# Experts loop: the rounding of the activated tile moves to ScalarE, its lower part moves one weight part later, and the positions of four experts are compared in one operation

## The reference, cut to what matters

```python
expert = grp[:, None] * EXPERTS_PER_GROUP + top_idx          # two experts for each token
h_pad = jnp.concatenate([h, jnp.zeros((1, d), h.dtype)], axis=0)
xb = h_pad[slot_tok].reshape(n_blocks, MOE_BLOCK, d)         # tokens gathered by expert
def run_block(args):
    xe, e = args
    return (jax.nn.silu(xe @ w_gate[e]) * (xe @ w_up[e])) @ w_down[e]
y = jnp.zeros((n_tok + 1, d)).at[slot_tok].add(yb * slot_gate[:, None])
```

## Time and profile before

| | us |
|---|---|
| three runs | 2054.73, 2055.91, 2060.94 |
| median | 2055.91 |
| span of the profiled execution | 2060.3 |
| busy in that span: PE, PEld | 1914.5, 1749.8 |
| busy in that span: DVE, ACT | 1423.0, 1168.0 |
| experts loop, first to last YE operation of passes 0 to 29 | 483.28 |

### The profile page before, as it was taken

One profiled execution on the slowest core, in us unless ns is written; L12 is line 12 of the kernel. 1 busy time (PEld: TensorE's weight loads), 2 busy tenths in 40 slices (PEclk: granted clock), 3 DMA queues, 4 the chain that ended last, 5 costly groups with the idle time before them and its releaser, 6 DMA issues.

```text
span 2060.3 us, 30308 instructions
## 1 busy us (share of the span) xinstructions
PE 1914.5 (93%) x12946; PEld 1749.8 (85%) x12946; DVE 1423.0 (69%) x1424; ACT 1168.0 (57%) x1310; POOL 76.5 (4%) x94
## 2 busy tenths in 40 slices
PE   6999998998998989998998999898789999999997
PEld 5989998997997979998997999796778888888785
DVE  4687548546555677637745555757679999999995
ACT  3553344544444554334644444465388888888883
POOL 0000013000000000013000000000000000000000
PEclk9999999998999999999998999999789999999998
DMA  8334374543554433356534555333269999999993
GB/s 307 121 116 149 128 255 164 205 143 143 186 183 144 159 144 133 131 179 237 213 139 150 184 184 184 139 117 122 111 256 376 377 377 377 372 380 372 374 396 131
DMA packets 64524, 440.87 MB, mean 214 GB/s; under 512 B 7372, under 2 KB 7372, under 8 KB 14592
## 3 DMA queue, kind: packets, MB, share of 16 engines
q1 hardware_dynamic: 55296, 399.63, 51.4%
q0 software_dynamic: 8096, 35.30, 4.7%
q10 hardware_dynamic: 992, 3.93, 0.5%
HBM read 428.61 MB, written 10.23 MB: 213 GB/s over the span
## 4 chain that ended last, share of the span: by engine, by line
PE 66%; DVE 21%; ACT 8%; issue 2%; POOL 1%; DMA 1%; DVEq 0%; ACTq 0%; POOLq 0%
PE psum L188 65%; DVE ring_low L202 6%; ACT hl L198 3%; DVE arena L212 3%; DVE ht L202 2%; DVE rounded L202 2%; DVE rounded L212 2%; PE psum L192 2%; DVE arena L202 1%; POOL arena L202 1%; ACT arena L198 1%; DVE hl L202 1%; ACT rounded L198 1%; ACT gn L198 1%; DVE resid L202 1%
## 5 line engine op out<-in xcount | busy, mean ns | idle before, releaser
L202 DVE TENSOR_TENSOR hl<-ring,hl 128x2048 fp32r<-128x2048 f32 (+1 forms) x190 | 433.7, 2286 | 316.7 <-ACT hl L198 316.3
L188 PE MATMUL psum<-ht,hl 128*128 128x256 f32 x4992 | 628.9, 287 | 7.5 <-DVE ht L202 7.5
L188 PEld LDWEIGHTS psum<-ht,hl 128*128 128x128 f32 x4992 | 614.6, 195 | 17.8 <-DVE ht L202 9.5
L198 ACT ACTIVATE hl<-ring 128x2048 fp32r<-128x2048 f32 (+1 forms) x286 | 536.4, 1895 | 116.9 <-PE psum L188 110.1
L198 ACT ACTIVATE arena<-psum 128x512 f32<-128x512 f32 (+5 forms) x232 | 120.9, 521 | 419.9 <-PE psum L188 395.3
L188 PE MATMUL psum<-hl,ax 128*128 128x512 f32 (+1 forms) x1608 | 351.9, 355 | 6.2 <-DVE ax L202 4.8
L188 PEld LDWEIGHTS psum<-hl,ax 128*128 128x128 f32 x1608 | 264.4, 191 | 47.5 <-DVE ax L202 5.5
L202 DVE TENSOR_TENSOR ring_low<-ring,hl 128x2048 fp32r<-128x2048 f32 x96 | 215.3, 2285 | 19.0 <-ACT hl L198 18.8
L188 PE MATMUL psum<-arena 128*128 128x128 f32 (+6 forms) x1520 | 190.1, 291 | 14.4 <-ACT arena L198 7.9
L188 PEld LDWEIGHTS psum<-arena 128*128 128x128 f32 (+2 forms) x1520 | 174.9, 180 | 25.1 <-ACT arena L198 8.7
L188 PE MATMUL psum<-hl,ht 128*128 128x256 f32 (+1 forms) x1056 | 138.4, 296 | 16.0 <-DVE ht L212 14.0
(11 more groups left out here) (121 smaller groups left out, 1890.1 us busy)
## 6 DMA issues: line engine op xcount, KB each, us to landing
ring<-W SPq DMA_DIRECT2D x284, 1024.0 KB, 5.1
arena<-W SPq DMA_DIRECT2D x48, 1024.0 KB, 7.8
ht_raw<-W SPq DMA_DIRECT2D x46, 1024.0 KB, 7.8
gate_d<-arena POOLq DMA_DIRECT2D x32, 256.0 KB, 3.8
arena<-gate_d POOLq DMA_DIRECT2D x8, 1024.0 KB, 9.3
gn<-GB POOLq DMA_DIRECT2D x10, 512.0 KB, 4.1
arena<-GB POOLq DMA_DIRECT2D x6, 512.0 KB, 5.1
ring<-W SPq DMA_DIRECT2D x4, 512.0 KB, 5.3
```

The costliest lines, as they stand in the source:

```text
L188: return Nothing() if self.e is None else self.e.matmul(o, a, b, start=start, stop=stop, skip_group_check=skip_group_check)
L198: return self.e.activation(o, a, f, bias=bias, scale=scale)
L202: return Nothing() if self.e is None else self.e.tensor_tensor(o, a, b, op)
```

## The change

Four edits, all in `few()` and its constants:

1. The copy that rounds hid into the upper part of aT leaves VectorE. ScalarE does it in a new step `upper_hid(e)` between the SE copy and the next two uppers. It waits for VectorE's "hid" of the same expert, and for TensorE's down(e-2).
2. The subtraction for the lower part of aT (`lower_hid`) moves on VectorE behind one more lower; it waits for ScalarE's new copy.
3. The wait for down(e-2) moves with the copy from VectorE to ScalarE.
4. `prep` becomes one operation of 128x1024 in place of four of 128x256. `iota` grows from 64 to 128 columns (the constants by 32 KB), and both of TensorE's waits are now for the end of the one operation.

```diff
-                   ("tri_ge", 128), ("iota", 64), ("fold", 64), ...
+                   ("tri_ge", 128), ("iota", 128), ("fold", 64), ...
...
-    put("iota", np.tile(np.arange(CAP, dtype=np.float32), (128, 1)))
+    put("iota", np.tile(np.arange(CAP, dtype=np.float32), (128, 2)))
...
-                    pe.wait_ge(s_dve, V["oh2", g])
+                    pe.wait_ge(s_dve, V["oh", g])
...
+                def upper_hid(e):
+                    ac.wait_ge(s_dve, V["hid", e])
+                    if e >= 2:
+                        ac.wait_ge(s_pe, P["ye", e - 2])
+                    act(mo.aT[e % 2][:, :, 0, :], mo.hid.rearrange("p (k n) -> p k n", k=4), ACT.Copy, "aT", e, after=False)
...
                     if e < 31:
                         place(e + 1)
+                    upper_hid(e)
                     cut(2)
...
-                    for s in range(2):
-                        for t in range(2):
-                            tt(mo.OH[g % 2][:, t, :].rearrange("p (e s n) -> p e s n", e=4, s=2)[:, :, s, :],
-                               posm[:, t, 4 * g:4 * g + 4].unsqueeze(2).broadcast_to([128, 4, 64]),
-                               C("iota").unsqueeze(1).broadcast_to([128, 4, 64]), ALU.is_equal, ("oh", "oh2")[s], g, after=False)
+                    tt(mo.OH[g % 2].rearrange("p t (e n) -> p t e n", e=4),
+                       posm[:, :, 4 * g:4 * g + 4].unsqueeze(3).broadcast_to([128, 2, 4, 128]),
+                       C("iota").unsqueeze(1).unsqueeze(1).broadcast_to([128, 2, 4, 128]), ALU.is_equal, "oh", g, after=False)
...
                 def turn_(e):
                     ve.wait_ge(s_act, A["sg", e])
                     tt(mo.hid, mo.sg, half(beside, 1), MUL, "hid", e)
-                    if e >= 2:
-                        ve.wait_ge(s_pe, P["ye", e - 2])
+
+                def lower_hid(e):
                     hi, lo = (mo.aT[e % 2][:, :, s, :] for s in range(2))
-                    hid = mo.hid.rearrange("p (k n) -> p k n", k=4)
-                    copy(hi, hid)
-                    tt(lo, hid, hi.bitcast(F32), SUB, "aT", e)
+                    ve.wait_ge(s_act, A["aT", e])
+                    tt(lo, mo.hid.rearrange("p (k n) -> p k n", k=4), hi.bitcast(F32), SUB, "aT", e, after=False)
...
                     turn_(e)
-                    cut(4)
+                    cut(1)
+                    lower_hid(e)
+                    cut(3)
```

More of the change, by code:

```diff
@@ L34 @@
 SHAPE_COLS = Cols([("ident", 128), ("rev", 128), ("rot", 128), ("bones", 128), ("ones", 128),
-                   ("tri_ge", 128), ("iota", 64), ("fold", 64), ("s_lt_t", 128), ("s_le_t", 128),
+                   ("tri_ge", 128), ("iota", 128), ("fold", 64), ("s_lt_t", 128), ("s_le_t", 128),
                    ("lev", 7 * 128), ("rowf", 2), ("eps6", 1), ("eps5", 1), ("eps64", 1), ("tiny", 1)])
```

## The result

| | before | after |
|---|---|---|
| median of 4 runs, us | 2058.43 | 2117.95 |
| lowest to highest | 2054.73 to 2062.27 | 2116.55 to 2119.86 |
| span of the profiled execution | 2060.3 | 2114.7 |
| YE operation of pass 0 to that of pass 29 | 483.28 | 537.89 |

The ratio is 1.0301 (95% interval 1.0283 to 1.0319): 59.5 us slower. Forecast were 57.5 slower and 2113.4, with a range of 2105 to 2129. Of the 23 runs of the kernel before that stand beside the last four variants, one took 6458.61 us; the ratios leave it out.

What follows compares the result with a forecast made beforehand. Bound: a circle of waits through TensorE's gather, ScalarE's copies and upper, VectorE's lowers and YE operation. Terms: 29 passes +52.5, pass 0 +2.4, pass 30 +2.1, first gather +0.45; together +57.5, 2113.4 us, range 2105 to 2129.

Steps and rivals of the forecast that it cites:

- hid at S+5.78, the stall, the hand-over: From YE operation start S: hid starts at 5.78, ScalarE stands about 2.1 us, hand-over from VectorE takes 0.04.
- The copy's price: ScalarE's new 128x256 copy rounding hid takes 0.26 us in its queue, with ends of 0 and 0.40.
- The plain pass: Experts-loop pass with gather and without prep, YE operation to YE operation: 18.31 us against 16.58, +1.73.
- With prep: Six passes in which prep stands ahead of hid: 18.31 + 1.15 = 19.46 us against 17.10.
- Without gather: Passes 27 to 29, bounded by VectorE's route to lower 12: 17.60 us against 15.79.
- The wide comparison: Prep's one operation of 1024 elements lasts 1.226 us, 1.15 in the queue, with ends of 0.9 and 1.4.
- What is next late: Slack beside the new circle: VectorE ready for lower 12 0.7 us early; TensorE needs about 16.25 of 18.31.
- Ahead of the loop: First gather waits for the whole wide prep operation, 1.23 us instead of about 0.77: about +0.45.
- a whole rival: TensorE's clock falls at new gaps; two falls a pass add 1.5 in 29 passes, total 2157; chance 0.09.
- a clock of 1.00 over the loop: Sign of a right forecast: TensorE's granted clock stays at 1.00 (2.4 GHz) throughout the experts loop.
- no stall: ScalarE finds hid done, if ready by S+4.5; plain passes stay 16.58, total 2053.3; chance 0.06.
- VectorE's work sets the pass: VectorE's work sets every pass; what it sheds, 17.3 us, comes off, giving 2038.6; chance 0.03.

Runs made afterwards that it cites:

- the last four variants: Hid one lower sooner 2058.99 us, prep as one operation only 2055.69, gu one upper later 2044.11, gather between the halves 2045.16; kernel before beside them 2057.81.
- lower part at once: The changed kernel with the lower part of aT right behind hid on VectorE, not one lower later: 2114.99 us.

## Why the prediction was right, point by point

- **hid at S+5.78, the stall, the hand-over.** In the changed kernel hid starts at 1743.63 with S at 1737.85: 5.78. The copy starts 0.04 after hid ends (1744.05 to 1744.09), the value taken from between 0.02 and 0.11. The profile puts the idle at 1.99, where the walk had 2.11 from the earliest next start; the rest is the SE copy's own tail.
- **The copy's price**, taken as 0.26 between 0 and 0.40: it is 0.32 from start to start (1744.09 to 1744.41). That term is 0.06 too small, and the whole pass came out only 0.03 longer than the sum.
- **The plain pass**, 18.31: measured 18.33 to 18.35. **With prep**, 19.46: 19.46 or 19.47. **Without gather**, 17.60: 17.64.
- **The wide comparison**, 1.226 less an overlap: it lasts 1.22 or 1.23, and broadcast operands make no difference.
- **What is next late.** VectorE at lower 12 was to wait 0.7; it waits 0.62. TensorE is off the circle with gaps of about 1 us before down, 0.8 before turn and 1.83 to 1.88 before down with prep; the forecast had 1.1 to 1.4, about 1, and 2.2 to 2.5.
- **Ahead of the loop.** The first gather starts 1.38 after the start of prep where it was 0.90, 0.48 later (forecast 0.45). From hid to the YE operation of pass 0 it is 12.63 (forecast 12.53).
- **The total.** Head apart (below), from the first operation of prep to the end it is 564.1 before (2060.3 - 1496.24) and 625.5 after (2114.7 - 1489.21): +61.4 where the terms summed to +57.5. The missing 3.9, all but 0.1 of it: plain passes 20 x 0.03 = 0.6; no gather 0.1; pass 1 with 18.95, 0.6; the pass behind prep three times 18.6, 0.8; pass 30, forecast 14.20 + 2.14 = 16.34, measured 17.89, 1.5; pass 31, 0.2.
- **The mis-sized term** is thus mainly the clock. I had counted its fall as a whole rival, twice in each pass, or as nothing, and named a clock of 1.00 over the loop as a sign of being right. Up to pass 30 it fell in a few single places: in pass 0, in three of the six passes with prep (15, 19 and 23), in pass 27, and in pass 30. The one in pass 0 isn't new: the kernel before has it too, and its pass 1 takes 17.14. TensorE's timeline and the window behind the prep of pass 15:

```profile
1805.27 0.47 PE L188 MATMUL psum<-hl,hx 128*128 128x512 f32 x1 [1.87 <-ACT rounded L198]
...
1805.81 0.59 PE L188 MATMUL psum<-hl,hx 128*128 128x512 f32 x1
1806.20 0.63 PE L188 MATMUL psum<-ring_low,hx 128*128 128x512 f32 x1
```
```profile
1804.00:1808.00 4.00, 2.73 (x8) 2.19 (x9) 3.40 (x4) 4.00 (x5) 0.00 (x0) 0.73 0.66 266
```

After the gap of 1.87 matmuls last 0.63 and start 0.43 apart for 3.4 us, at 1.2 GHz, then 0.40 and 0.23 apart again. In the other three passes with prep, behind gaps of 1.83 to 1.88, the clock stayed at 1.00. The Trainium skill, TensorE: Matmul & The Clock Gate, section HAM oscillation, has a loop that loses its clock in each iteration behind a long wait; here, with shorter gaps, it did so in a few passes only. The length of a gap doesn't tell which: gaps of 1.87 and 1.82 before down in passes 28 and 29 left the clock at 1.00, while in pass 27 it fell behind a gap of 0.81 before turn, and the variant with hid one lower sooner lost it once, behind one of 0.77. What decides is open.

What a fall costs depends on whether TensorE is on the circle. In pass 27 it cost nothing (17.64, as the two passes behind it), behind prep 0.25, in pass 30 1.5, and in the variant with hid sooner, whose passes go through TensorE's gather, 1.5 (18.19 for 16.65). That the falls lengthen the passes behind prep is shown by three kernels, the changed one, prep as four operations and lower part at once: of their 18 passes that follow one with prep, nine come behind a fall and take 18.59 to 18.61, and nine come behind none and take 18.34 to 18.36.

For pass 30 there is a pair: the variant with prep as four operations has the same work and the same gap before down(30), 1.81 against 1.83, but there the clock held, and the pass took 16.34, the forecast's value. Windows behind that gap, of the changed kernel and then of the variant:

```profile
2082.00:2084.00 2.00, 2.00 (x7) 1.56 (x6) 1.32 (x1) 0.00 (x0) 0.00 (x0) 0.58 0.00 0
2084.00:2086.00 2.00, 2.00 (x7) 1.57 (x6) 0.00 (x0) 0.00 (x0) 0.00 (x0) 0.57 0.00 0
```
```profile
2088.00:2090.00 2.00, 2.00 (x10) 1.60 (x9) 1.02 (x1) 0.00 (x0) 0.00 (x0) 1.00 0.00 0
```
- **The rival "no stall"** had its point of decision right: with hid ready at S+4.21 there is no loss. One step in it was wrong. I held that passes without gather can't fall under 15.8 because DMA was at a share of 1.00. With less on VectorE they are 15.26 to 15.38 in the two versions with the copy behind the uppers, at a share of 1.01 and more GB/s. Nor do the passes with prep fall to 16.6: they take 16.90 with the copy behind two uppers and 17.28 with hid one lower sooner, for prep delays hid. The window of a pass without gather, from the kernel with the copy behind two uppers:

```profile
1983.69:1999.05 15.36, 15.36 (x78) 12.64 (x77) 15.26 (x11) 14.38 (x14) 0.00 (x0) 1.00 1.01 418
```

- **The rival "VectorE's work sets the pass"** holds in those three passes, where 0.45 of its 0.52 came off until TensorE was full (15.36 of 15.36), and for the 0.2 that prep in one operation gives in the six passes with it. In plain passes the relief is worth nothing with the copy behind the uppers, and with it in front the wait makes them 1.7 us longer. The Trainium skill, Perfetto Trace Analysis, section Identifying the Most-Contended Engine, would have had the fuller of VectorE and ScalarE relieved first; the plain passes do not bear the rule out here.
- **Where I said the profiled execution of before was among the three times**: a fourth run, of 2062.27, has since been listed, and the span of 2060.3 fits that one, not the median. The forecast on the median carried the difference over unchanged, so nothing hung on it.

## What to carry to other kernels

A step that is moved to another engine brings its wait with it, and everything behind that wait in the engine's queue is delayed, needed or not: compare the time at which the value is ready with the time at which the queue gets there, and put the step at the first place where the value is already there. When all engines are nearly full, work out the circle of waits, step by step through the queues, before counting what an engine sheds; what is on the circle pays in full, what is off it is free until it becomes the circle. And look for steps that stand in front of a critical one only by program order: moving the gu copy behind one upper took 0.4 us off every plain pass, more than VectorE was relieved of by giving the cast away (0.3).

## What the runs showed of the hardware

The head of the program, before the experts, was 7.0 us shorter in the changed kernel's profiled execution (first prep operation at 1489.21 instead of 1496.24), with the same instructions but for the larger constant load. Windows of the kernel before from 40 to 55 us, and then of the changed kernel:

```profile
40.00:45.00 5.00, 3.79 (x18) 3.79 (x19) 4.71 (x7) 4.72 (x7) 0.00 (x0) 0.63 0.92 376
45.00:50.00 5.00, 5.00 (x26) 5.00 (x25) 3.47 (x2) 0.89 (x1) 0.00 (x0) 0.50 0.55 201
50.00:55.00 5.00, 5.00 (x40) 4.87 (x40) 0.18 (x1) 1.91 (x3) 0.00 (x0) 0.51 0.58 236
```
```profile
40.00:45.00 5.00, 4.35 (x39) 4.35 (x40) 4.71 (x7) 4.82 (x6) 0.00 (x0) 1.00 0.84 345
45.00:50.00 5.00, 5.00 (x77) 4.84 (x75) 3.09 (x3) 2.25 (x4) 0.00 (x0) 1.00 0.64 231
50.00:55.00 5.00, 5.00 (x34) 4.48 (x35) 3.80 (x10) 3.56 (x15) 0.00 (x0) 1.00 0.48 193
```

In that one execution TensorE ran at half its clock for over 10 us, behind a wait of 1.98 where the changed kernel's had 1.41; in the other nine profiled executions of this study the clock was 1.00 there. The whole 7.0 us is there soon after: VectorE's first reciprocal of 128x4 starts at 75.82 instead of 68.82, and at 68.8 to 70.1 in the other eight. The rest of the head varies too: in the nine executions without this fall the first prep operation starts between 1489.21 and 1493.71, and the changed kernel's is the earliest. So single spans differ by 7 us for a reason far away from the change, and comparing the profiled spans alone would have given +54.4 for a change that cost 59.5. The lengths of single passes, which repeat to 0.03 us where the clock holds, are the better measure.
